# One sequence of heads through two attention mixers: own latent key tiles, two buffers of scaled queries and keys, rotated keys written in VectorE's waits

## The reference, cut to what matters

```python
# layers 0 and 1 ("A"): sliding-window attention, pooling, latent attention
out_a = swa_mixer(q_a, k_a, v_a, ...)      # 6 heads of 64, window 128, sinks, relative bias
out_b = pool_mixer(u_b, ...)
out_c = mla_mixer(cq_c, ckv_c, kr_c, ...)  # 6 heads: 64 plain + 32 rotated features, causal
x = x + concatenate([out_a, out_b, out_c]) @ w_out[l]
x = x + (silu(h @ w_gate[l]) * (h @ w_up[l])) @ w_down[l]
# layer 2 ("R"): a linear recurrence, and 4 heads of cross-attention into 256 memory tokens
# layer 3 ("F"): fox_group (8 causal heads of 64 with a forget term), then the same cross-attention
x = x + concatenate([y_mix, y_mem], axis=-1) @ w_out[layer]
x = x + square(relu(rms_norm(x) @ w1)) @ w2
```

## Time and profile before

| what | value |
|---|---|
| time, median of 3 runs | 2462.72 us (2459.45 to 2465.17) |
| the profiled execution, its own time | 2461.81 us |
| its span in the profile | 2460.0 us |
| TensorE busy | 2325.4 us, 95% of the span |
| VectorE, ScalarE, GpSimd busy | 42%, 20%, 68% |
| TensorE's mean granted clock | 0.976 of full |

### The profile page before, as it was taken

How to read it: one execution, slowest core, us unless ns; L and a number is a source line. 1 busy time by engine, 2 the same in 40 slices (tenths; PEclk the granted TensorE clock), 3 DMA queues, 4 the chain that set the end, 5 groups by cost and what they waited for, 6 DMA issues and landing times.

```text
span 2460.0 us, 29677 instructions
## 1 busy us (share of the span) xinstructions
PE 2325.4 (95%) x11024; PEld 1897.5 (77%) x11024; DVE 1027.3 (42%) x1302; ACT 501.6 (20%) x955; POOL 1669.6 (68%) x1378
## 2 busy tenths in 40 slices
PE   6988999999997899999998699999999798999999
PEld 4776888888776688888887478888888676888887
DVE  7654533422465253332237645215334334540430
ACT  3244211110124421111012411001111263100000
POOL 5565777777656577777777677667766566776774
PEclk9989999999998999999999899999999999999999
DMA  4200222222320022222232112222232210222222
GB/s 164 100 18 18 86 102 87 100 83 94 123 91 18 18 86 101 87 102 82 94 130 93 45 70 103 94 94 102 87 118 86 86 35 18 90 99 102 88 100 86
DMA packets 37892, 207.93 MB, mean 85 GB/s; under 512 B 3580, under 2 KB 10364, under 8 KB 16936
## 3 DMA queue, kind: packets, MB, share of 16 engines
q1 hardware_dynamic: 37800, 206.70, 23.9%
HBM read 204.55 MB, written 2.13 MB: 84 GB/s over the span
## 4 chain that ended last, share of the span: by engine, by line
PE 60%; POOL 3%; DVE 2%; ACT 2%; issue 2%; DMA 0%; DVEq 0%; POOLq 0%; ACTq 0%; SPq 0%
PE ps L855 18%; PE ps L859 18%; PE ps L860 18%; POOL wl L654 2%; PE ps L1231 1%; PE ps L1205 1%; ACT rt L1379 1%; PE ps L1246 0%; DMA raw<-w_in_f 0%; POOL wh L649 0%; PE ps L1209 0%; PE ps L1206 0%; PE ps L1207 0%; POOL act L739 0%; DVE sq L1749 0%
## 5 line engine op out<-in xcount | busy, mean ns | idle before, releaser
L654 POOL TENSOR_TENSOR wl<-raw,wh 128x512 fp32r<-128x512 f32 (+1 forms) x776 | 1030.6, 1360 | 0.2
L649 POOL TENSOR_SCALAR wh<-raw 128x1024 fp32r<-128x1024 f32 (+1 forms) x388 | 428.1, 1123 | 583.6 <-PE ps L855 459.4
L855 PE MATMUL ps<-h,wh 128*128 128x512 f32 x1576 | 618.2, 392 | 25.5 <-DVE h L1757 18.5
L860 PE MATMUL ps<-h,wl 128*128 128x512 f32 x1576 | 614.3, 390 | 0.0
L859 PE MATMUL ps<-h,wh 128*128 128x512 f32 x1576 | 614.2, 390 | 0.0
L855 PE MATMUL ps<-act,wh 128*128 128x512 f32 x1120 | 438.0, 391 | 1.1 <-DVE x L1749 1.1
L859 PE MATMUL ps<-act,wh 128*128 128x512 f32 x1120 | 436.2, 389 | 0.0
L860 PE MATMUL ps<-act,wl 128*128 128x512 f32 x1120 | 435.8, 389 | 0.0
L855 PEld LDWEIGHTS ps<-h,wh 128*128 128x128 f32 x1576 | 296.2, 188 | 94.5 <-issue 28.9
L860 PEld LDWEIGHTS ps<-h,wl 128*128 128x128 f32 x1576 | 296.4, 188 | 61.8
L859 PEld LDWEIGHTS ps<-h,wh 128*128 128x128 f32 x1576 | 296.4, 188 | 61.7 <-issue 1.0
(11 more groups left out here) (326 smaller groups left out, 2671.4 us busy)
## 6 DMA issues: line engine op xcount, KB each, us to landing
raw<-w_gu SPq DMA_DIRECT2D x44, 1024.0 KB, 4.8
raw<-w_up SPq DMA_DIRECT2D x32, 1024.0 KB, 4.9
raw<-w_down_b SPq DMA_DIRECT2D x32, 1024.0 KB, 4.8
raw<-w_down_a SPq DMA_DIRECT2D x32, 704.0 KB, 4.0
raw<-w_in_a SPq DMA_DIRECT2D x14, 1024.0 KB, 4.9
raw<-w_in_f SPq DMA_DIRECT2D x13, 1024.0 KB, 4.9
raw<-w_in_r SPq DMA_DIRECT2D x11, 1024.0 KB, 4.9
raw<-w_out_a SPq DMA_DIRECT2D x8, 1024.0 KB, 8.2
```

What stands on the lines that cost most here:

```text
L649: pool.tensor_scalar(hi_s[:, part], raw[s][:, part], 1.0, 1.0, ALU.mult, ALU.mult).then_inc(hi_done, 1)
L654: return pool.tensor_tensor(lo_s[:, part], raw[s][:, part], hi_s[:, part].bitcast(F32), ALU.subtract)
L855: first = pe.matmul(out, w_hi, v_hi, start=start, stop=False)
L860: return pe.matmul(out, w_lo, v_hi, start=False, stop=stop)
```

## The change

Both mixers of a layer become one list of heads. `attention(seq)` replaces two calls of `attention(m)` on all four engines; a step g works on `order[g]`, whatever mixer it belongs to, and `begins(seq)` says at which step a unit is prepared: the second mixer's first two units at the first mixer's last two steps. `m.use(b, u)` gives the count of a bank's uses over the whole list.

- mla has its own two key tiles `key_mla` (in the place of `swq` and `swk`, which are read by then), an own second diagonal tile `dg1_mla`, and the query slots in the opposite order.
- the scaled queries and keys have two buffers, `t[:, 0:2]` and `t[:, 2:4]`; VectorE's `prep` waits for GpSimd's remainders of the unit before the last one.
- the shared rotated key is scaled at step 2 (`ROTATE_AT`) and written into `key_mla[0]` at step 2 and `key_mla[1]` at step 3, in `rotation(g)`. TensorE's spread for it moves to step 2.
- VectorE's `prep` and `rotation` stand in `meanwhile()`, called in `out` between the sink's sum and the wait for the reciprocal; before, `prep` stood ahead of `out`.
- in F the two weight chunks are split at steps 2 and 4 instead of 4 and 7; in A at steps 3 and 9 (swa's 3 and mla's 3, as before); in R at 2 and 4, as before.

```diff
     def slot(self, u):
-        return u % 2
+        return (u + (self.name == "mla")) % 2
@@
+def begins(seq):
+    at, first = {}, 0
+    for i, m in enumerate(seq):
+        if i:
+            at[first - 2], at[first - 1] = (m, 0), (m, 1)
+        for hd in range(m.heads):
+            if m.starts(hd):
+                at[first + hd] = (m, m.starts(hd))
+        first += m.heads
+    return at
@@ tiles
-        key_pairs = {"swa": [[key[0], key[1]]], "mla": [[key[0]], [key[1]]], "xa": [[key[0]], [key[1]]],
+        key_mla = [view(f"key_mla{s}", A_AT + 32768 + 29696 + s * 4096, [2, T], F32R) for s in range(2)]
+        key_pairs = {"swa": [[key[0], key[1]]], "mla": [[key_mla[0]], [key_mla[1]]], "xa": [[key[0]], [key[1]]],
@@
-        dgs = {"swa": (dg0, dg1_swa), "mla": (dg0, dg1), "fox": (dg0, dg1), "xa": (dg0, dg1)}
+        dg1_mla = view("dg1_mla", A_AT + 32768 + 45056, [TB, P], F32R)
+        dgs = {"swa": (dg0, dg1_swa), "mla": (dg0, dg1_mla), "fox": (dg0, dg1), "xa": (dg0, dg1)}
@@
+        normed = [(t[:, 2 * i, :], t[:, 2 * i + 1, :]) for i in range(2)]
@@ GpSimd
-                    attention(SWA, MLA, 3)
-                    attention(MLA, second_at=3, slot_done=7)
+                    attention((SWA, MLA), {3: None, 9: (7, 2)})
@@
-                    attention(FOX, XA, 4, second_at=7, slot_done=0)
-                    attention(XA)
+                    attention((FOX, XA_F), {2: None, 4: (0, -1)})
@@ TensorE
-                for hd in range(m.heads + 1):
-                    if hd + 1 < m.heads:
-                        score_rows(hd + 1, 0)
-                    if m.starts(hd):
-                        prep(m, m.starts(hd))
-                    if hd < m.heads:
-                        score_columns(hd)
...
-                    if hd == m.heads:
-                        bk.close(m.early())
-                        if nxt:
-                            start(nxt)
-                    if hd:
-                        weighted(hd - 1)
+                for g in range(n + 1):
+                    if g + 1 < n:
+                        score_rows(*order[g + 1], 0)
+                    if g in at:
+                        m, u = at[g]
+                        if u == 0 and m.name == "xa":
+                            start(m)
+                        else:
+                            prep(m, u)
+                    if seq[-1].name == "mla" and g == ROTATE_AT:
+                        rotation()
+                    if g < n:
+                        score_columns(*order[g])
+                    if seq[0].name == "swa" and g < 2:
+                        pooled(s_pool, g)
+                    if g + 1 < n:
+                        score_rows(*order[g + 1], 1)
+                    if g:
+                        weighted(*order[g - 1])
@@ ScalarE
+                for g in range(n + 2):
+                    if g >= 2:
+                        reciprocal(*order[g - 2])
+                    if g + 1 < n:
+                        diagonals(*order[g + 1], 0)
+                    if g < n:
+                        exponentials(*order[g])
+                    if g in at:
+                        prep(*at[g], order[g])
+                    if g + 1 < n:
+                        diagonals(*order[g + 1], 1)
@@ VectorE, prep
-                if nqk.n:
-                    dve.wait_ge(qk_ready, nqk.at())
+                if nqk.n >= 2:
+                    dve.wait_ge(qk_ready, nqk.at(-1))
@@ VectorE
-                if m.name == "mla":
-                    dve.wait_ge(ready[7], bk.filled(7, 0))
-                    r = slice(64, P)
-                    tt(ts[r, :], krp[r, :], ps[7][r, :], ALU.mult, bk.empties(7, 0))
-                    for s in range(2):
-                        split(ts[r, :], key[s][r, 0, :], key[s][r, 1, :], chain)
+            def rotation(g):
+                r = slice(64, P)
+                if g == ROTATE_AT:
+                    b, u = 7, MLA.use(7, 0)
+                    dve.wait_ge(ready[b], bk.filled(b, u))
+                    tt(ts[r, :], krp[r, :], ps[b][r, :], ALU.mult, bk.empties(b, u))
+                both = key_mla[g - ROTATE_AT]
+                split(ts[r, :], both[r, 0, :], both[r, 1, :], chain)
@@
-            def out(hd):
+            def out(m, hd, meanwhile):
...
-                dve.wait_ge(ready[4], bk.filled(4, hd))
                 if m.name == "swa":
+                    dve.wait_ge(ready[4], bk.filled(4, hd))
                     dve.wait_ge(free[5], bk.emptied(5, hd))
                     tt(es[s, :], ps[4][s, :], es[s, :], ALU.add, den)
+                meanwhile()
+                dve.wait_ge(ready[4], bk.filled(4, m.use(4, hd)))
                 dve.wait_ge(recip_ready, rec.up())
```

More of the change, by code:

```diff
@@ L199, with __init__ @@
 class Mixer:
-    def __init__(self, kind, name, heads, per_unit, rows, scale, tile0, place, kidx):
+    def __init__(self, kind, name, heads, per_unit, rows, scale, tile0, place, kidx, after=None):
         self.kind, self.name, self.heads, self.per_unit = kind, name, heads, per_unit
@@ L205, in __init__, with use @@
         self.units = heads // per_unit
+        self.earlier = after.uses() if after else {}
+    def use(self, b, u):
+        return self.earlier.get(b, 0) + u
     def unit(self, h):
@@ new lines, in attention, with finished @@
+            def attention(seq, chunks_at, recurrence=False):
+                order, at = heads_of(seq), begins(seq)
+                n = len(order)
+                def finished(g):
+                    m, hd = order[g - 2]
+                    mixed(m.vrow(hd), m.tile(hd))
+                prep(seq[0], 1)
+                for g in range(n + 2):
+                    if g in at:
+                        prep(*at[g])
+                    cross = order[min(g, n - 1)][0].name == "xa"
+                    if cross:
+                        if g >= 2:
+                            finished(g)
+                        if g < n:
+                            summed(*order[g])
+                    if g in chunks_at:
+                        split_all(1, BLOCKS, chunks_at[g])
+                    if g == n and seq[-1].name == "mla":
@@ L782, in attention @@
                         for j in range(2):
                             mixed(slice(0, P), 3 + j, up[:, j, :])
-                    if hd >= 2 and m.name != "xa":
-                        mixed(m.vrow(hd - 2), m.tile(hd - 2))
-                    if hd == m.heads and nxt:
-                        prep(nxt, 0)
-                    if recurrence and hd < 4:
-                        mixed(slice(0, P), hd)
-                bk.close(m.uses())
+                    if g >= 2 and not cross:
+                        finished(g)
@@ L792, in _ @@
+                    if recurrence and g < 4:
+                        mixed(slice(0, P), g)
+                for m in seq:
+                    bk.close(m.uses())
             s = 0
@@ L1685, in _ @@
                     in_a()
[L1686 to L1687 removed]
+                    attention((SWA, MLA), l)
                     if l == 0:
@@ L2184, in out, with meanwhile @@
                         dve.sem_inc(free[5], 1)
[L2186 to L2212 removed]
+                order, at = heads_of(seq), begins(seq)
+                n = len(order)
+                maxima(*order[0], 0)
+                prep(seq[0], l, 1)
+                maxima(*order[0], 1)
+                if seq[0].name == "swa":
+                    head_stat(5, -1, T, 1)
+                for g in range(n + 2):
+                    if g + 1 < n:
+                        maxima(*order[g + 1], 0)
+                    if seq[-1].name == "mla" and g == n:
+                        mixs.n += 2
+                    def meanwhile():
+                        if g in at:
+                            prep(at[g][0], l, at[g][1])
+                        if seq[-1].name == "mla" and g in (ROTATE_AT, ROTATE_AT + 1):
+                            rotation(g)
+                    if g >= 2:
+                        out(*order[g - 2], meanwhile)
+                    else:
+                        meanwhile()
+                    if g + 1 < n:
+                        maxima(*order[g + 1], 1)
+                    if seq[0].name == "swa" and g < 2:
+                        pooled(l, g)
+                    if layers[l] == "R" and g < 4:
+                        recurrence(g)
+                for m in seq:
+                    bk.close(m.uses())
             def resid(gains):
```

248 lines of the change are left out of this document (105 added, 143 removed).

## The result

The changed kernel takes 2426.32 us (median of 4 runs, 2419.74 to 2433.67) where the kernel before takes 2463.28 (4 runs beside them): a ratio of 0.985, 95% interval 0.9833 to 0.9866. The forecast was 2427. The profiled execution took 2427.67 us, its span is 2425.9.

What follows compares the result with a forecast made beforehand. TensorE, busy 95% of the span, was taken as the bound, with gains only where it idles or runs slow in the mixers: 25.7 + 0 + 9.5 + 0 = 35.2 us off, so 2427 us, range 2415 to 2442.

Steps and rivals of the forecast that it cites:

- The join of layers 0 and 1: From swa head 3's score columns to mla head 2's, 50.1 us before: five steps forecast, 12.9 us gained per layer.
- The two waits on `pt`: TensorE in mla's first two columns, waiting behind the reciprocals of swa 4 and 5: 1.4 us each.
- that on `key_mla`: TensorE's wait for ScalarE's `key` ahead of mla's first score rows: 0.5 us.
- The full clock in the join: TensorE at full clock from swa head 3 to mla head 2, where the old join had 0.61 in its slow stretch.
- wait near 3.07 us: In the old swa-to-mla join, TensorE waited 3.07 us for VectorE's rotated keys; the low clock followed.
- Rival 4: Slower: waits of 1.4 us in joined steps keep TensorE at 1.2 GHz; 2507, or 2467 with three steps; chance 0.05.
- The moved vector work: VectorE's `prep` and `rotation` in the swa steps: costs and savings cancel to 0, bounds -2.6 to +0.7 us per layer.
- The second buffer: VectorE's `prep` for swa's third unit no longer waits for GpSimd behind the pooling work: 0 to 0.7 us per layer.
- The last layer: Join from fox to cross-attention (xa), fox 7's columns to xa 1's and on: 9.5 us gained, bounds 6 to 10.5.
- the wait of 1.70 us: Last layer, fox's `weighted` waiting for `sq`: put down to GpSimd's second split holding `mixed` and VectorE's `out`.
- The recurrent layer: One mixer in the same order, TensorE waiting for VectorE's unmoved recurrence: 0 gained, bounds -1 to +1 us.

## Why the prediction was right, point by point

**The join of layers 0 and 1** was right in sum and, within 0.6 us, in each of its steps. Forecast 6.5, 7.0, 7.0, 8.2, 8.65 us; measured 7.11, 7.34, 6.51, 7.63, 8.22; 37.3 against 36.81. The two waits on `pt` came where they were put and were 0.98 instead of 1.4; that on `key_mla` was 0.39 instead of 0.5. Gained 13.3 and 13.6 us, forecast 12.9. Of the stretches outside the join, layer 0's were 1.3 us quicker and layer 1's 1.0 slower.

**The full clock in the join** was right, its reason too weak. I argued that no wait near 3.07 us was left. Waits of 1.71 and 1.80 us were enough in other kernels, and 1.47 at the end of this one. What held was that the join kept to 0.98 us and below. The waits of 1.4 that I had forecast stood close to the 1.47 us behind which it fell. Rival 4 had a chance of 0.05, and one line's place apart from the kernel the clock did fall in the joined steps (53.76 us for the join).

**The moved vector work** at nothing was right for the order in the change. Step 3 took 0.64 and 1.66 us where an undisturbed step took 0.42 and 0.69: 1.2 us over, inside the bounds of 0 to 1.9. What I left out is what it covers: in the place ahead of `es` the same work costs 34 us.

**The second buffer** was mis-sized. I gave it 0 to 0.7 us a layer, as half of a `prep`; it is 5.4 us in the two joins (4.9 in the median), by a GpSimd queue that I had named ("behind the pooling work") but not followed to TensorE. The sum came out all the same: the join of the changed kernel has the second buffer in it, and I had built that join's steps without any such wait.

**The last layer**: forecast 9.5 us, measured 7.8. Up to xa 1 it was right: the two steps ahead of fox 7 are 1.35 us longer, with work of xa in them (1.3 forecast), and fox 7 to xa 1 takes 12.23 us (12.4). Behind xa 1 I had assumed the old order and time; it took 21.54 us against 19.31, because the next step is 5.47 against 4.99 and the last weighted values, behind the same wait of 2.14 us, take 3.22 us against 1.98 at a lower clock. The step that failed is a cause: that GpSimd's split held `mixed` and so made the wait of 1.70 us. It was the pipeline's drain. The size came out all the same because the single sequence removes a drain as well. And the place of the splits, which I had put at that wait, is worth 6.5 us here for another reason: left late, GpSimd would have held the joined heads.

**The recurrent layer** was unchanged, as forecast (54 us there: TensorE 33.34 busy, VectorE 38.76).

**The total** came within a microsecond (2427 against 2426.32), and that close is luck: layers 0 and 1 gained 27.2 us where 25.7 were forecast, the last layer 7.8 where 9.5 were, and the recurrent stretch took 0.8 more. The four runs alone lie 14 us apart.

## What to carry to other kernels

Price a wait on a matrix engine that is otherwise full at its own length and, here from about 1.5 us on, a possible toll of 1.5 to 2.5 us for the clock behind it. The toll was not paid each time: up to 3.7 us a wait of one length cost it in one place and not in another. So joining two pipelines is worth more than the waits that it removes, and the order of two small operations on a side engine can be worth the whole change. Put moved work behind the operation that starts another engine, not ahead of it, and look at what a counting wait really asks for: where one count covers several kinds of work, moving one kind makes others wait.

## What the hardware showed that I had not expected

- The clock of TensorE fell to or near 1.2 GHz behind single waits of 1.47 us (0.57 in the stretch behind), 1.71 (0.53), 1.80 (0.54), 4.06 (0.63) and 9.86 (0.52). The fourteen traces have 246 waits of 0.89 us or more that began at full clock in the stretches around the mixers of layers 0, 1 and 3 (96 to 256, 712 to 872 and 1928 to 2088 us). Where the granted clock in the stretch right behind is below 0.97, I call it a fall. Behind all 72 of 0.89 to 1.44 us the clock stayed at full. Behind the 88 of 1.47 to 2.23 us it fell 35 times, behind all 59 of 2.32 to 3.51 us, behind 11 of the 14 of 3.70 to 3.72, and behind all 13 of 4.05 to 9.86. So between 1.47 and 3.72 us the length does not settle it, and what does stays open. One of the three that held, in the kernel with the late splits:

```profile
216.35 2.42 PE L1271 MATMUL ps<-pt_a,vom 128*128 128x512 f32 x8 [3.71 <-DVE sq L1795]
```

- VectorE operations that read SBUF alone were stretched beside GpSimd again and again, by about one microsecond and to nearly the same value: 0.69 to 1.65 or 1.66 us, and the first split operation from 0.42 to 1.47 in the kernel with the work ahead of the sum. The added products of 0.69 took 0.90 on average over 12 and 1.24 over 4. The Trainium skill, page "SBUF — State Buffer", section "Who interferes with whom", has an exclusive lock for a whole instruction there; by it I had estimated 2.5 us for the two operations of step 3. They took 1.2 us over, and 2.0 in the other kernel: the kind agrees, the size depends on how the two meet.
